# An RG-LRU layer worked block by block: its gates placed between the projections of its gelu branch, tanh in place of sigmoid, the convolution's first taps issued earlier

## The reference, cut to what matters

```python
proj = h @ w_in                                  # 1024 x 2048
y, u = split(proj, [1024])
y = gelu(y)
uc = conv_b + sum(u_pad[:, tap:tap+S] * cw[tap] for tap in range(4))
ub = uc.reshape(B, S, 4, 256)                    # 4 blocks of 256 channels
r  = sigmoid(einsum('bsnc,ncd->bsnd', ub, wa) + ba)
ig = sigmoid(einsum('bsnc,ncd->bsnd', ub, wx) + bx)
log_a = -8 * r * softplus(-lam)
a = exp(log_a)
b_in = sqrt(-expm1(2 * log_a)) * (ig * uc)
hs = scan of h[t] = a[t] * h[t-1] + b_in[t]      # over the 256 tokens
out = (hs * y) @ w_out                           # 1024 x 1024
```

## Time and profile before

| | |
|---|---|
| median of 3 runs | 1273.69 us |
| the profiled execution | 1272.74 us, its span 1271.5 us |
| granted TensorE clock, mean | 0.98 |
| TensorE matmuls busy | 1210.7 us (95%) |
| VectorE, ScalarE, GpSimd busy | 693.1 (55%), 586.1 (46%), 461.6 us (36%) |
| the third layer in the span, first matmul of `lu` to the end of its output product | 968.0 to 1075.0 us |

### The profile page before, as it was taken

How to read it: one execution, slowest core, us unless ns; L and a number is a source line. 1 busy time by engine, 2 the same in 40 slices (tenths; PEclk the granted TensorE clock), 3 DMA queues, 4 the chain that set the end, 5 groups by cost and what they waited for, 6 DMA issues and landing times.

```text
span 1271.5 us, 19815 instructions
## 1 busy us (share of the span) xinstructions
PE 1210.7 (95%) x8341; PEld 1111.2 (87%) x8341; DVE 693.1 (55%) x984; ACT 586.1 (46%) x896; POOL 461.6 (36%) x252
## 2 busy tenths in 40 slices
PE   6979999999998999999999999999999769999998
PEld 6978888788887999988889879999888768999986
DVE  5654554347676653432779865543326696643423
ACT  6434344454444543443663344444435674544432
POOL 3333233323332244443274521544432440544441
PEclk9889999999999999999999999999999979999999
DMA  8644264534444476665444345655555434665560
GB/s 248 189 134 132 76 196 124 146 100 133 133 133 146 153 214 181 185 194 185 147 147 142 117 148 160 206 183 185 195 184 154 161 118 132 191 191 182 183 198 34
DMA packets 156721, 202.12 MB, mean 159 GB/s; under 512 B 13407, under 2 KB 131337, under 8 KB 156633
## 3 DMA queue, kind: packets, MB, share of 16 engines
q1 hardware_dynamic: 154792, 194.21, 49.6%
q0 software_dynamic: 1840, 6.64, 1.6%
HBM read 199.76 MB, written 1.07 MB: 158 GB/s over the span
## 4 chain that ended last, share of the span: by engine, by line
PE 80%; DVE 10%; ACT 6%; issue 2%; DMA 0%; POOL 0%; SPq 0%; DVEq 0%; ACTq 0%; POOLq 0%
PE bank L474 15%; PE bank L480 15%; PE bank L477 15%; PE bank L491 9%; PE bank L497 9%; PE bank L494 9%; PE bank L823 2%; ACT whi L924 2%; DVE wlo L1327 2%; DVE sm L1623 1%; DVE ring L1625 1%; DVE uc L1453 1%; DVE ring L1611 1%; DVE hn L1579 1%; PE bank L769 1%
## 5 line engine op out<-in xcount | busy, mean ns | idle before, releaser
L1864 POOL TENSOR_TENSOR wlo<-raw,whi 128x1024 fp32r<-128x1024 f32 x159 | 404.0, 2543 | 577.6 <-ACT whi L924 577.5
L924 ACT ACTIVATE whi<-raw 128x1024 fp32r<-128x1024 f32 x368 | 364.8, 1041 | 122.6 <-PE bank L497 118.0
L1327 DVE TENSOR_TENSOR wlo<-raw,whi 128x1024 fp32r<-128x1024 f32 x209 | 274.7, 1325 | 258.7 <-ACT whi L924 257.8
L474 PE MATMUL bank<-hh,whi 128*128 128x256 f32 x1808 | 296.7, 286 | 2.9 <-ACT hh L956 1.7
L477 PE MATMUL bank<-hh,wlo 128*128 128x256 f32 x1808 | 292.6, 284 | 7.3 <-DVE wlo L1327 7.3
L480 PE MATMUL bank<-hl,whi 128*128 128x256 f32 x1808 | 292.1, 284 | 0.4 <-DVE hl L1446 0.4
L474 PEld LDWEIGHTS bank<-hh,whi 128*128 128x128 f32 x1808 | 251.4, 193 | 11.9 <-issue 10.8
L477 PEld LDWEIGHTS bank<-hh,wlo 128*128 128x128 f32 x1808 | 251.1, 193 | 7.7 <-DVE wlo L1327 7.7
L480 PEld LDWEIGHTS bank<-hl,whi 128*128 128x128 f32 x1808 | 251.0, 193 | 0.6 <-DVE hl L1446 0.6
L491 PE MATMUL bank<-whi,gh 128*128 128x512 f32 x264 | 83.4, 397 | 0.0
L497 PE MATMUL bank<-whi,gl 128*128 128x512 f32 x264 | 83.1, 395 | 0.0
(11 more groups left out here) (296 smaller groups left out, 1345.1 us busy)
## 6 DMA issues: line engine op xcount, KB each, us to landing
raw<-in_ffn_w_in SPq DMA_DIRECT2D x88, 512.0 KB, 3.6
raw<-in_w_in SPq DMA_DIRECT2D x72, 512.0 KB, 3.7
raw<-in_ffn_w_out SPq DMA_DIRECT2D x44, 512.0 KB, 3.4
raw<-in_hgrn_w_in SPq DMA_DIRECT2D x32, 512.0 KB, 4.1
raw<-in_w_ffn_gate SPq DMA_DIRECT2D x22, 512.0 KB, 4.3
raw<-in_w_ffn_up SPq DMA_DIRECT2D x22, 512.0 KB, 4.1
raw<-in_w_ffn_down SPq DMA_DIRECT2D x22, 512.0 KB, 3.3
raw<-in_w_branch SPq DMA_DIRECT2D x16, 512.0 KB, 4.2
```

What stands on the lines that cost most here:

```text
L474: T.matmul(out, wh[:, i, c], xh[:, k, :], start=first and (i, k) == pairs[0], stop=False)
L924: A.activation(half_of(whi, j, h), half_of(raw, j, h), ACT.Copy).then_inc(s_hi[j % NS][h], 1)
L1327: V.tensor_tensor(half_of(wlo, j, h), half_of(raw, j, h), half_of(whi, j, h).bitcast(f32), ALU.subtract).then_inc(s_lo[j % NS][h], 1)
L1864: G.tensor_tensor(half_of(wlo, j, 1), half_of(raw, j, 1), half_of(whi, j, 1).bitcast(f32), ALU.subtract).then_inc(s_lo[j % NS][1], 1)
```

## The change

The four blocks of 256 channels are worked one at a time. The gates of one block (24 matmuls) now stand in TensorE's order as: `ly0`, gates 0, gates 1, `ly1`, `ly2`, gates 2, `ly3`, gates 3, output product; the unit `lg1` is loaded one place later, behind `ly2`. Sigmoid(v) is written (1 + tanh(v/2))/2. The added halves go into the constants, into a scale 0.25 of the square root, and into `input_factor`, which on VectorE now also makes `(ig + 1) * uc` in place of GpSimd's four multiplications. ScalarE and VectorE issue the steps in another order, and of the output product the last two units instead of three are worked first for s = 0.

```diff
@@ order of the units, of TensorE
         cols(("ly", 1), lw, 256, 256)
+        cols(("ly", 2), lw, 512, 256)
         lru_gate_unit(1)
-        cols(("ly", 2), lw, 512, 256)
...
-                for n in range(n_units - 3):
+                for n in range(n_units - tail):
...
             project_columns(("ly", 0), 6)
             lru_gates(0)
+            lru_gates(1)
             project_columns(("ly", 1), 6)
-            lru_gates(1)
             project_columns(("ly", 2), 6)
+            lru_gates(2)
             project_columns(("ly", 3), 6)
+            lru_gates(3)
             rot_banks[0] = [0, 1, 2, 3]
-            add_product(("lo",), 4, ch, cl, lambda k: (s_hs, k // 2 + 1), lambda k: (s_hs, k // 2 + 1), 7)
+            add_product(("lo",), 4, ch, cl, lambda k: (s_hs, k // 2 + 1), lambda k: (s_hs, k // 2 + 1), 7, tail=2)
@@ ScalarE
+            def lru_gates(n):
+
                 for i, (dst, b0) in enumerate(((ig, 88), (rg, 80))):
...
+                    aq.wait_ge(*full("lg", i, n))
+                    aq.wait_ge(s_vec, 1)
+                    for dd in range(2):
+                        c = 2 * n + dd
+                        t = A.activation(dst[:, c, :], bank_of("lg", i, n)[:, 256 * dd:256 * dd + 256], ACT.Tanh, scale=0.5,
+                                         bias=vec[:, b0 + c:b0 + c + 1])
+                    t.then_inc(evacuated("lg", i, n), 1)
+                aq.wait_ge(*evac("lg", 1, n))
+                for c in (2 * n, 2 * n + 1):
+                    A.activation(aT[:, c, :], rg[:, c, :], ACT.Exp, scale=vec[:, 96 + c:97 + c], bias=vec[:, 96 + c:97 + c])
+                    t = A.activation(th[:, c, :], rg[:, c, :], ACT.Tanh, scale=vec[:, 120 + c:121 + c], bias=vec[:, 120 + c:121 + c])
+                t.then_inc(s_aa, 1)
...
-                A.activation(rg[:, sl, :], rg[:, sl, :], ACT.Sqrt).then_inc(s_root, 1)
+                A.activation(rg[:, sl, :], rg[:, sl, :], ACT.Sqrt, scale=0.25).then_inc(s_root, 1)
...
+            conv_start(0)
+            conv_start(1)
             use(("lu", 2))
-            conv_unit(0)
+            conv_round(0)
+            conv_start(2)
             use(("lu", 3))
-            conv_unit(1)
+            conv_round(1)
+            conv_start(3)
             use(("ly", 0))
+            use(("lg", 0))
             lru_gates(0)
-            conv_unit(2)
-            conv_unit(3)
             use(("ly", 1))
+            conv_round(2)
             lru_gates(1)
             use(("ly", 2))
-            for n in range(4):
-                root_of(n)
+            conv_round(3)
+            root_of(0)
+            root_of(1)
+            use(("lg", 1))
             use(("ly", 3))
             for n in range(4):
-                gated(n)
+                gelu(n)
+            gated(0)
+            gated(1)
+            use(("lo", 0))
+            lru_gates(2)
+            lru_gates(3)
+            use(("lo", 1))
+            root_of(2)
+            root_of(3)
+            gated(2)
+            gated(3)
             add_product(("lo",), 4, 7)
@@ VectorE
-            V.tensor_scalar(lam, cst[:, 0, :], -8.0, None, ALU.mult)
-            V.tensor_scalar(vec[:, 120:128], cst[:, 0, :], 8.0, None, ALU.mult).then_inc(s_vec, 1)
+            V.tensor_scalar(lam, cst[:, 0, :], -4.0, None, ALU.mult)
+            V.tensor_scalar(vec[:, 80:96], vec[:, 80:96], 0.5, None, ALU.mult)
+            V.tensor_scalar(vec[:, 120:128], cst[:, 0, :], 4.0, None, ALU.mult).then_inc(s_vec, 1)
...
-                vq.wait_ge(s_aa, 2 * n + 2)
+                vq.wait_ge(s_aa, n + 1)
+                V.scalar_tensor_tensor(ig[:, sl, :], ig[:, sl, :], 1.0, uc[:, sl, :], ALU.add, ALU.mult)
...
+            conv_unit(0)
             use(("lu", 2))
             u_of(2)
-            conv_unit(0)
+            conv_unit(1)
             use(("lu", 3))
             u_of(3)
-            conv_unit(1)
             use(("ly", 0))
+            conv_unit(2)
             y_of(0)
             use(("lg", 0))
-            conv_unit(2)
+            use(("ly", 1))
+            y_of(1)
             conv_unit(3)
+            use(("ly", 2))
             input_factor(0)
             input_factor(1)
...
+            y_of(2)
             use(("lg", 1))
+            scan(0)
+            scan(1)
+            y_of(3)
+            use(("ly", 3))
+            gated(0)
+            gated(1)
+            use(("lo", 0))
             input_factor(2)
             input_factor(3)
...
+            use(("lo", 1))
             scan(2)
-            gated(0)
-            gated(1)
             scan(3)
             gated(2)
             gated(3)
@@ GpSimd
-            def gated_input(h):
...
-            gated_input(1)
-            use(("ly", 3))
+            use(("lo", 0))
             add_product(("lo",), 4, 7)
```

More of the change, by code:

```diff
@@ L560, in project_pair, with add_product @@
                         transposes(1, e)
-            def add_product(key, n_units, xh, xl, hi, lo, e, by_token=False, before_last=None):
+            def add_product(key, n_units, xh, xl, hi, lo, e, by_token=False, before_last=None, tail=3):
                 halves = halves_of(by_token)
@@ L578, in part @@
                         used[j, 0] = used[j, 1] = (s_full[7], turns["add", e, 1, 1][2] - n_units + n + 1)
-                for n in range(n_units - 3):
+                for n in range(n_units - tail):
                     part(n, 0)
                     part(n, 1)
-                for n in range(n_units - 3, n_units):
+                for n in range(n_units - tail, n_units):
                     if before_last is not None and n == n_units - 2:
@@ L875, in tensor_program @@
             feed_forward(1, 5, 6)
-            def lru_gates(h):
-                u = unit_at["lg", h]
+            def lru_gates(n):
+                u, z = unit_at["lg", n // 2], n % 2
                 wh, wl = whole(whi, u), whole(wlo, u)
                 for i in range(2):
[L882 to L896, removed]
+                    b = turn(("lg", i, n), next_bank())
+                    tq.wait_ge(*hi_set(u, z))
+                    tq.wait_ge(*lo_set(u, z))
+                    tq.wait_ge(s_ucl, n + 1)
+                    tq.wait_ge(*free(("lg", i, n)))
+                    for dd in range(2):
+                        c, out = slice(256 * i + 128 * dd, 256 * i + 128 * dd + 128), banks[b][:, 256 * dd:256 * dd + 256]
+                        for k in (2 * n, 2 * n + 1):
+                            w = 2 * z + k % 2
+                            T.matmul(out, wh[:, w, c], ch[:, k, :], start=k == 2 * n, stop=False)
+                            T.matmul(out, wh[:, w, c], cl[:, k, :], start=False, stop=False)
+                            tok = T.matmul(out, wl[:, w, c], ch[:, k, :], start=False, stop=k == 2 * n + 1)
+                    tok.then_inc(s_full[b], 1)
+                used[u, z] = full("lg", 1, n)
             project_pair([("lu", 0), ("lu", 1)], 6)
@@ L1800, in scan @@
                 vq.wait_ge(s_root, n + 1)
-                vq.wait_ge(s_ti, n + 1)
                 vq.wait_ge(*own.mark(V.tensor_tensor(rg[:, sl, :], rg[:, sl, :], ig[:, sl, :], ALU.mult)))
```

37 lines of the change are left out of this document (3 added, 34 removed).

## The result

The changed kernel took 1278.47 us (median of 8 runs, 1276.9 to 1280.87), the kernel before beside it 1273.97 (8 runs). The ratio is 1.0036, with a 95% interval of 1.0025 to 1.0046: slower by 4.5 us, where +3.6 was forecast. Its profiled execution has a span of 1276.2 us, 4.7 more than before; the clock is 0.982.

What follows compares the result with a forecast made beforehand. TensorE, 95% busy, was taken as bound, time winnable only in its waits and low clock. Product end 1078.6 against 1074.96 gave +3.6: 1272.74 to 1276.3 us profiled, 1277.3 as median; 8 in 10 range 1268 to 1281.5.

Steps and rivals of the forecast that it cites:

- hold at `ly2`: TensorE waits 4.7 us at `ly2` for VectorE's split, done at 1016.2; the earlier 6.8 us hold moves there.
- T: Time of VectorE's first `yg * ig`: 1041.8 us, against 1048.32 before; TensorE begins the output product 2.2 us later.
- second hold: Within the output product, before part (2, 0), TensorE waits 6.7 us for `cl` of block 2.
- The walk: Step-by-step timing of the new order across the engines, from 982.4 us to the product's end at 1078.6.
- the second half decides: Late inputs of blocks 2 and 3 stretch the output product to 34.6 us from 24.4, ending 3.6 us later.
- GpSimd's splits shut VectorE out in full: Each 2.35 us GpSimd split blocks VectorE operations without a PSUM operand until its end, and the reverse.
- faster: Rival: GpSimd hardly delays VectorE, no hold at `ly2`, product ends 5.8 us earlier, 1267.9 us; chance 0.14.
- no change: Rival: part of VectorE's waits is hidden, product ends 0.7 us earlier, 1273.0 us; chance 0.14.
- The clock rival: Rival: low TensorE clock lasts longer from `ly2` to gates 3, or at second slow start; +6 to +9.5 us; chance 0.12.
- the hold of 0.6 us ahead of the gates of block 0: TensorE wants the split of `lg0` at 998.86 but gets it at 999.3: about 0.6 us, no more.
- 1.9 for a second slow start: Low clock when the output product resumes with block 2 costs 1.9 us, within 13.6 us to its end.
- The sigmoids as tanh cost the same each: Among the small parts: on ScalarE, each sigmoid written as tanh costs the same.

Runs made afterwards that it cites:

- gates23_ahead: Changed kernel with ScalarE's gate functions of blocks 2 and 3, and VectorE's factors for them, moved earlier, gates ahead of the gelus; 1271.59 us, 0.9993 of the kernel before.
- no_pool_splits: Changed kernel with VectorE in place of GpSimd making the second low halves of units `lu3` to `lo1`; 1275.11 us, 1.0014 of the kernel before.
- before_bias: Kernel before with only a bias column added to the exp and tanh of the decay, which changes the decay's value; ran once, 1277.92 us.
- ly2_split_first: Changed kernel with VectorE's low split of `ly2` moved ahead of the convolution of block 2; 1278.27 us, 1.0035 of the kernel before.
- all_gates_first: Changed kernel, all gates, then four roots, then gelus; factors 2, 3 before scans, `lo3` splits last, `ly2` low split before block 2's taps; 1273.28 us, 0.9997 of before.
- tail_three: Changed kernel with `tail=2` taken back: three units of the output product worked first for s = 0; 1280.55 us, 1.0058 of the kernel before.

## Why the prediction was right

| step | as predicted | in the trace |
|---|---|---|
| hold at `ly2` | 4.7 us, the low half done at 1016.2 | 4.69, matmul at 1016.07 |
| clock behind it | 4 us low, off the chain | 3.3 us low; no piece of TensorE in the chain |
| T, first `yg * ig` | 1041.8 | 1041.42 |
| product starts | 1044.0 | 1043.63 |
| wait for bank 6 | a little over 1 us | 0.89 |
| root of block 2 set | T + 16.7 | T + 17.5 |
| VectorE through with the splits of `lo3` | T + 17.2 | T + 17.9 |
| product goes on with block 2 | T + 23.2 | T + 23.9 |
| second hold | 6.7 us | 8.05 |
| from there to the end | 13.6 | 14.3 |
| product ends | 1078.6 | 1079.62 |

The walk held within 0.5 us up to the product, and its two claims were tested apart. That the second half decides: gates23_ahead, −6.9 us (−5.5 by the ratios). That GpSimd's splits shut VectorE out in full: the rows of the taps and of `cl` (5.18 and 2.42 us), and no_pool_splits, −3.4 us, although VectorE took on their work; were they only to slow each other now and then, that work would have made it slower. The two rivals that rested on fewer shut-outs, "faster" and "no change", fall with this. The clock rival falls too: behind the hold at `ly2` the low clock lasted 3.3 us, off the chain.

The end came 1.0 us later than computed: T −0.4, block 2 +0.7, the last stretch +0.7. So 0.4 us of it is luck: from T on the walk is 1.4 us short. And the hold of 0.6 us ahead of the gates of block 0 isn't in the trace (TensorE stands still for 0.29 us there, at 999.16); nothing hung on it. The mis-sized terms are two. I priced exp and tanh at the 0.40 us of the earlier trace rows, but the change also gives them a bias column, and then it is 0.49 to 0.50 (before_bias): eight of them in the second half are the 0.7 to 0.8 us by which the root of block 2 and VectorE's factor of block 3 are late. And "1.9 for a second slow start" was 2.5: the twelve matmuls from 1065.29 to 1070.53 us took 5.24, where 12 by 0.227 is 2.72; the rest of the 0.7 is a tenth here and there. The second hold is 1.35 us longer than forecast, half of it for block 2 being late and half because TensorE was out of work 0.7 us sooner.

"The sigmoids as tanh cost the same each" holds, but the prediction took the tanh form for neutral. By itself it is +2.5 us, through VectorE's added operations beside GpSimd's splits; the walk did carry them (1.2 us in the chain for blocks 0 and 1), and did not ask what the order of before would have done with them. How the +4.5 us divides among the parts stays open: they don't add up one by one, and the later place of `lg1` and TensorE's new order were never run alone.

Of the 6.9 us that the product starts earlier, then, nothing reached the end: ScalarE's gates of blocks 2 and 3 were paid behind it, as a hold, as a second slow start, and partly with `tail=2` covering it.

## What to carry to other kernels

An early start of a long product is worth nothing when its later inputs come later: look at when the last input is ready, and put an engine's work for the late blocks ahead of the early blocks' finish where the product can't run through otherwise (6.9 us here). Before moving work from GpSimd to VectorE, or ordering a chain through VectorE, look which GpSimd operations run beside it; handing VectorE the GpSimd splits as well lowered the median in all five orders tried, by 0.6 to 7.5 us, clearly in two (5.3 and 7.5) and in a third with intervals that touch (3.4). Ask the chain before removing a hold of TensorE: it is worth it only if what releases the last input waits for that engine. A hold of 4.3 us at `ly3` was off the chain in one order (ly2_split_first) and on it in another (all_gates_first).

## What the runs showed of the hardware

- A bias column beside a scale column costs a 256-element exp or tanh 0.09 to 0.10 us (0.40 to 0.49 or 0.50 from one to the next).
- Two programs that differ only in the order of the parts had the product begin at the low clock behind much the same hold (9.11 and 9.28 us). In one execution it lasted 3 us (1043.63 to 1046.6, after), in the other 9.5 (1044.97 to 1054.5, tail_three), with 0.89 us of standing still early in both.
- The granted clock can fall within a hold, ahead of any matmul: in the hold from 1034.5 to 1043.63 us of the kernel after it is 1.00 until 1039.5 and 0.50 from 1040.
- Two GpSimd splits in a row (5.05 us) held up two taps of VectorE for 4.2 us: 5.18 us for the pair, where it takes 1.00 alone; and the two splits themselves took 0.35 us longer than two of 2.35.
- A table load took 1.28 us, and the first function stood right behind it each time (1048.12 and 1049.41; 1056.96 and 1058.26). "ScalarE: Activation LUTs" of the Trainium skill (what ACT_TABLE_LOAD costs) adds a drain of about 1380 ns; these rows too show none.
